# Key/value block of a two-layer trunk: all eight weight slabs fetched at once, products by feature group

## The reference

```python
def rms_norm(x, g):
    y = x * lax.rsqrt(jnp.mean(x * x, axis=-1, keepdims=True) + NORM_EPS)
    return y * g

a = rms_norm(h, g[0])                      # h = x, (256, 2048)
qkv = a @ w_qkv                            # (2048, 2048 + 256 + 256)
q = qkv[..., :2048]; k = qkv[..., 2048:2304]; v = qkv[..., 2304:]
# sliding-window attention with sinks, @ w_o, added to h; then a squared-ReLU MLP;
# layer 1: a gated MLP over chunks, added to h; then a squared-ReLU MLP
```

## Time and profile before

| | |
|---|---|
| median of 3 runs | 1972.24 us (1971.83 to 1972.36) |
| the profiled execution's span | 1971.5 us |
| PE busy | 1949.2 us, 99% of the span, 8914 products and transposes |
| PE weight loads | 1604.2 us, 81% |
| DVE busy / ACT busy | 1076.2 us (55%) / 972.2 us (49%) |
| granted TensorE clock, mean | 0.997 |
| moved by DMA | 368.40 MB, 187 GB/s on average |

### The profile page before, as it was taken

How to read it: one execution, slowest core, us unless ns; L and a number is a source line. 1 busy time by engine, 2 the same in 40 slices (tenths; PEclk the granted TensorE clock), 3 DMA queues, 4 the chain that set the end, 5 groups by cost and what they waited for, 6 DMA issues and landing times.

```text
span 1971.5 us, 26643 instructions
## 1 busy us (share of the span) xinstructions
PE 1949.2 (99%) x8914; PEld 1604.2 (81%) x8914; DVE 1076.2 (55%) x1276; ACT 972.2 (49%) x1339; POOL 6.2 (0%) x23
## 2 busy tenths in 40 slices
PE   7999999999999999999999999999999999999998
PEld 5777888888888888888888888888888888888886
DVE  5666575454454455455667655654544554544455
ACT  6666465435434543454564445654355435434542
POOL 0000000000000000000000000000000000000000
PEclk9999999999999999999999999999999999999999
DMA  6634656555555555555475555565555555555553
GB/s 205 203 128 164 207 197 203 191 192 182 191 195 180 189 192 192 192 172 196 150 259 171 192 189 177 173 212 199 194 177 188 196 191 190 178 199 189 182 192 107
DMA packets 189833, 368.40 MB, mean 187 GB/s; under 512 B 12616, under 2 KB 12752, under 8 KB 189008
## 3 DMA queue, kind: packets, MB, share of 16 engines
q1 hardware_dynamic: 187264, 360.75, 54.8%
q0 software_dynamic: 1040, 6.82, 0.9%
q10 hardware_dynamic: 1472, 0.08, 0.0%
HBM read 365.51 MB, written 2.10 MB: 186 GB/s over the span
## 4 chain that ended last, share of the span: by engine, by line
PE 98%; DMA 1%; ACT 0%; DVE 0%; SPq 0%; issue 0%; DVEq 0%; ACTq 0%
PE acc L357 31%; PE acc L359 31%; PE acc L358 31%; PE t L378 2%; DMA w_raw<-in_attn_w_qkv 1%; PE t L391 1%; PE scores L459 0%; PE o L481 0%; PE t L469 0%; PE scores L591 0%; PE t L439 0%; ACT a_hi L650 0%; DVE w_lo L977 0%; DVE h L1014 0%; ACT w_hi L630 0%
## 5 line engine op out<-in xcount | busy, mean ns | idle before, releaser
L977 DVE TENSOR_TENSOR w_lo<-w_raw,w_hi 128x1024 fp32r<-128x1024 f32 x680 | 820.6, 1224 | 632.1 <-ACT w_hi L630 603.5
L630 ACT ACTIVATE w_hi<-w_raw 128x1024 fp32r<-128x1024 f32 x680 | 708.4, 1058 | 626.0 <-PE acc L359 590.9
L357 PE MATMUL acc<-w_hi,a_hi 128*128 128x512 f32 x1440 | 573.5, 398 | 4.8 <-DVE w_lo L977 4.4
L359 PE MATMUL acc<-w_hi,a_lo 128*128 128x512 f32 x1440 | 563.2, 391 | 0.0
L358 PE MATMUL acc<-w_lo,a_hi 128*128 128x512 f32 x1440 | 562.5, 391 | 0.0
L357 PE MATMUL acc<-w_hi,b_hi 128*128 128x512 f32 x1280 | 500.9, 391 | 0.0
L359 PE MATMUL acc<-w_hi,b_lo 128*128 128x512 f32 x1280 | 498.4, 389 | 0.0
L358 PE MATMUL acc<-w_lo,b_hi 128*128 128x512 f32 x1280 | 498.1, 389 | 0.0
L357 PEld LDWEIGHTS acc<-w_hi,a_hi 128*128 128x128 f32 x1440 | 271.3, 188 | 62.2 <-issue 7.5
L359 PEld LDWEIGHTS acc<-w_hi,a_lo 128*128 128x128 f32 x1440 | 271.2, 188 | 58.3
L358 PEld LDWEIGHTS acc<-w_lo,a_hi 128*128 128x128 f32 x1440 | 271.6, 189 | 53.5
(11 more groups left out here) (120 smaller groups left out, 475.6 us busy)
## 6 DMA issues: line engine op xcount, KB each, us to landing
w_raw<-in_mlp_w_up SPq DMA_DIRECT2D x256, 512.0 KB, 4.2
w_raw<-in_mlp_w_down SPq DMA_DIRECT2D x256, 512.0 KB, 4.4
w_raw<-in_sgu_w_in SPq DMA_DIRECT2D x64, 512.0 KB, 4.6
w_raw<-in_attn_w_qkv SPq DMA_DIRECT2D x40, 512.0 KB, 4.6
w_raw<-in_attn_w_o SPq DMA_DIRECT2D x32, 512.0 KB, 4.2
w_raw<-in_sgu_w_out SPq DMA_DIRECT2D x32, 512.0 KB, 4.4
gain<-in_norm_gains POOLq DMA_DIRECT2D x4, 1024.0 KB, 5.4
h<-in_x SPq DMA_DIRECT2D x8, 256.0 KB, 11.4
```

The costliest lines, as they stand in the source:

```text
L357: nc.tensor.matmul(acc[t][:, :], lhsT=x_hi[:, kb, tok], rhs=w1, start=(kb == 0), stop=False)
L359: last = nc.tensor.matmul(acc[t][:, :], lhsT=x_lo[:, kb, tok], rhs=w1, start=False, stop=(kb == KB - 1))
L630: nc.scalar.activation(w_hi[:, i % SLOTS, :], w_raw[:, i % RAW_SLOTS, :], ACT.Copy).then_inc(hi_made, 1)
L977: nc.vector.tensor_tensor(w_lo[:, i % SLOTS, :], w_raw[:, i % RAW_SLOTS, :], w_hi[:, i % SLOTS, :].bitcast(F32), ALU.subtract).then_inc(lo ...
```

## The change

In the key/value block alone:

- Slabs 4 to 7 go to four slots in y (kv_raw) with four semaphores of their own (kv_landed). SP issues all 16 transfers, x units and slabs in turn, with no wait. Query slabs 0 to 3 then wait for DVE's low part of key/value slabs 0 to 3.
- Units come by feature group, both halves of a group one after the other (X_UNIT). PE multiplies, for each pair, both its slabs with t 0, then both with t 1, with the next group's two transposes after the second and the third slab half.
- ACT and DVE take unit i, slab i, for i from 0 to 7. Only then come ACT's four squares, each followed by the split of a query slab (0 to 3), the root, kv_evac(0), query slab 4, kv_evac(1), query slab 5. DVE's sum for the norm stands behind query slab 3's low part.
- The branches for layer 0 in `first_block` go; the other blocks keep their order.

The diff, without the branches that go:

```diff
+X_UNIT = [(pair, t) for pair in range(NB) for t in range(TOK)]
...
+        kv_raw = yf[:, :].rearrange("p (i n) -> p i n", i=RAW_SLOTS)
...
+        kv_landed = [sem(f"kv_landed{i}") for i in range(RAW_SLOTS)]
...
+        def raw(blk, i):
+            if isinstance(blk, int) and blk == B_KV and i >= RAW_SLOTS:
+                return kv_raw[:, i - RAW_SLOTS, :]
+            return w_raw[:, i % RAW_SLOTS, :]
...
             def load_x(n):
-                pair, t = UNIT[n]
+                pair, t = X_UNIT[n]
...
-            for units, slabs in (([0], (0, 2)), ([1], (2, 3)), ([2, 3], (3, 4)), ([4], (4, 6)), ([5, 6, 7], (6, 8))):
-                for n in units:
-                    load_x(n)
-                load_block(B_KV, w_qkv[0], D, slabs=range(*slabs))
-            with sp.Fori(0, NB) as j:
+            for i in range(2 * PAIRS):
+                load_x(i)
+                sp.dma_start(raw(B_KV, i).rearrange("p (k n) -> p k n", k=SLAB_KB), kv_source(i)
+                             ).then_inc(slab_landed[i] if i < RAW_SLOTS else kv_landed[i - RAW_SLOTS], 16)
+            for i in range(RAW_SLOTS):
+                sp.wait_ge(lo_made, i + 1)
+                src = w_qkv[0].rearrange("(k p) n -> p k n", p=P)[:, i * SLAB_KB:(i + 1) * SLAB_KB, 0:COL]
+                sp.dma_start(w_raw[:, i, :].rearrange("p (k n) -> p k n", k=SLAB_KB), src).then_inc(slab_landed[i], 16)
+            load_block(B_Q, w_qkv[0], 0, slabs=range(RAW_SLOTS, 2 * PAIRS))
+            with sp.Fori(1, NB) as j:
                 load_block(j + B_Q, w_qkv[0], j * COL)
...
+            def kv_block():
+                transpose_unit(0, 0, True)
+                transpose_unit(1, 0, True)
+                for pair in range(PAIRS):
+                    for t in range(TOK):
+                        for i in (2 * pair, 2 * pair + 1):
+                            pe.wait_ge(t_lo, X_UNIT.index((pair, t)) * 4 + (i % 2 + 1) * SLAB_KB)
+                            multiply_slab(B_KV, a_hi, a_lo, i, t)
+                            if pair < PAIRS - 1 and (t, i % 2) in ((0, 1), (1, 0)):
+                                transpose_unit(2 * pair + 2 + t, 0, True)
...
-            first_block(B_KV, 0, first_layer=True)
+            kv_block()
...
+            def kv_block(evac):
+                for i in range(2 * PAIRS):
+                    split_unit(i, 0, 0, X_UNIT)
+                    split_slab(B_KV, i)
+                for i, (t, part) in zip((2, 3, 4, 5), ((0, 0), (1, 0), (0, 1), (1, 1))):
+                    for pair in (2 * part, 2 * part + 1):
+                        act.wait_ge(x_landed[X_UNIT.index((pair, t))], 16)
+                    square_h(t, part)
+                    split_next(B_KV, i)
+                take_root()
+                act.wait_ge(norm_done, norms[0])
+                evac(0)
+                split_next(B_KV, 6)
+                evac(1)
+                split_next(B_KV, 7)
...
-            first_block(B_KV, 0, 0, kv_evac, layer0=True)
+            kv_block(kv_evac)
...
+            def kv_block():
+                for i in range(2 * PAIRS):
+                    split_unit(i, 0, 0, X_UNIT)
+                    split_slab(B_KV, i)
+                split_next(B_KV, 2, 3, 4, 5)
+                input_norm()
+                rotary_angles()
+                split_next(B_KV, 6, 7)
...
-            first_block(B_KV, 0, 0, layer0=True)
+            kv_block()
```

More of the change, by code:

```diff
@@ L381, in transpose_unit @@
             def transpose_unit(n, use0, first_layer=False):
-                pair, t = UNIT[n]
+                pair, t = X_UNIT[n] if first_layer else UNIT[n]
                 if first_layer:
@@ L421, in first_block @@
                     if step in units:
-                        transpose_unit(units[step], use0, first_layer)
-                h_base[0] += 0 if first_layer else UNITS
+                        transpose_unit(units[step], use0)
+                h_base[0] += UNITS
             h_base = [0]
@@ L625, in split_slab @@
             def split_slab(blk, i):
-                act.wait_ge(slab_landed[i % RAW_SLOTS],
-                            blk * (32 * PAIRS // RAW_SLOTS) + 16 * (i // RAW_SLOTS + 1))
+                if not isinstance(blk, int) or blk > B_KV:
+                    act.wait_ge(slab_landed[i % RAW_SLOTS],
+                                blk * (32 * PAIRS // RAW_SLOTS) + 16 * (i // RAW_SLOTS))
+                elif i < RAW_SLOTS:
+                    act.wait_ge(slab_landed[i], 16)
+                else:
+                    act.wait_ge(kv_landed[i - RAW_SLOTS], 16)
                 at_least(act, slab_used, blk * (2 * PAIRS) + (i + 1 - SLOTS))
[L630 to L634, removed]
+                nc.scalar.activation(w_hi[:, i % SLOTS, :], raw(blk, i), ACT.Copy).then_inc(hi_made, 1)
             def split_next(blk, *slabs):
@@ L642, in split_ahead, with split_unit @@
                 split_next(blk, 2 * pair, 2 * pair + 1)
-            def split_unit(n, use0, norm):
-                pair, t = UNIT[n]
+            def split_unit(n, use0, norm, order=UNIT):
+                pair, t = order[n]
                 act.wait_ge(t_filled, use0 + n + 1)
@@ L675, in first_block @@
+            def first_block(blk, use0, norm, evac):
                 h0 = h_seen[0]
-                h_seen[0] += 0 if layer0 else UNITS
+                h_seen[0] += UNITS
                 def square(t, part):
[L679 to L684, removed]
-                    square_h(t, part)
@@ L687, in first_block @@
[L687 to L691, removed]
+                    act.wait_ge(h_ready, h0 + UNIT.index((2 * part + 1, t)) + 1)
+                    square_h(t, part)
                 split_unit(2, use0, norm)
[L693 to L696, removed]
+                split_ahead(blk - 1, 3)
@@ L711, in first_block @@
                 square(1, 1)
-                if not layer0:
-                    split_next(blk, 3)
+                split_next(blk, 3)
                 take_root()
@@ L976, in split_slab @@
                 dve.wait_ge(hi_made, blk * (2 * PAIRS) + (i + 1))
-                nc.vector.tensor_tensor(w_lo[:, i % SLOTS, :], w_raw[:, i % RAW_SLOTS, :],
+                nc.vector.tensor_tensor(w_lo[:, i % SLOTS, :], raw(blk, i),
                                         w_hi[:, i % SLOTS, :].bitcast(F32), ALU.subtract).then_inc(lo_made, 1)
-            def split_slabs(blk, pair):
-                for i in (2 * pair, 2 * pair + 1):
-                    split_slab(blk, i)
             def split_next(blk, *slabs):
@@ L1026, in inverse, with input_norm @@
                 nc.vector.reciprocal(dst[:, tok], root[:, tok]).then_inc(norm_done, 1)
[L1028 to L1060, removed]
+            def input_norm():
                 sums[0] += 2 * TOK
@@ L1065, in first_block @@
                 inverse(r_in)
-                if layer0:
-                    rotary_angles()
+            def kv_block():
[6 more added lines that the diff above has]
+                split_next(B_KV, 6, 7)
+            def first_block(blk, use0, norm):
+                split_unit(2, use0, norm)
+                split_ahead(blk - 1, 3)
+                update_h(4)
+                split_unit(3, use0, norm)
+                update_h(5)
+                split_unit(4, use0, norm)
+                update_h(6)
+                split_next(blk, 0)
+                split_unit(5, use0, norm)
+                split_next(blk, 1)
+                update_h(7)
+                split_unit(6, use0, norm)
+                split_next(blk, 2)
+                split_unit(7, use0, norm)
+                split_next(blk, 3)
+                input_norm()
                 split_ahead(blk, 2)
```

18 lines of the change are left out of this document (7 added, 11 removed).

## The result

The changed kernel takes 1977.81 us (median of 9 runs) against 1972.24 for the kernel before (9 runs): 5.6 us more, a ratio of 1.0028 with a 95% interval of 1.0019 to 1.0037. Forecast were 1978.2 us, with 1975.4 to 1981.2 as the range. The profiled execution spans 1977.7 us, 6.2 more than before. A time is 1.8 us above its execution's span (1979.53 for the 1977.7 here), so the profiled executions lie above their medians, by 1.7 us after, as the longest of the 9, and by 1.1 us before.

A forecast was written before the change was run, and what follows sets the result against it. TensorE was taken to bound the kernel, the query block's start being what the change can move. Starting 3.6 us later plus 2.4 us of fallen clock gives +6.0: 1978.2 us, range 1975.4 to 1981.2.

The forecast's parts named there:

- The anchor: Key/value block: slab 3 lands at 20.7 us again and PE takes it at 23.1, so this start doesn't move.
- the transfers' part: Part 1, key/value block: removing SP's waits for slabs 4 to 7 is worth nothing.
- Case (d): Transfers come earlier without SP's waits, slab 3 starts at 21.3 us, not 23.1: +4.2, 1976.4 us; chance 0.08.
- The loop: Part 2, key/value block: transposes, units and slabs take 7.7 us a pair against PE's 6.3, so PE waits 1.4 in each.
- evac(0): ACT's step that frees acc 0 for the query block: starts at 47.6 us, after squares, query splits and norm.
- The clock: Part 4: PE's clock falls once, at the wait before the query block, costing 2.4 us at half rate.
- the prediction's own sign: Granted clock near 0.6 in 45 to 50 or 50 to 55 and 1.00 in 25:30; below 1 in both is (b).
- rival (b): The clock falls both times, also at the wait before slab 3: +8.2, 1980.4 us; chance 0.20.
- The sum: Whole kernel: 3.6 us later query block plus 2.4 of clock, +6.0; span 1977.5, time 1978.2 us; chance 0.52.
- part 3: ACT frees acc 0 at 48.7 us; the query block starts at 48.8, 3.6 later, after a 6.2 us PE wait.
- Rival (a): The clock stays at its upper level through the 6.2 us wait before the query block: +3.6, 1975.8 us; chance 0.15.
- (c): evac(0) isn't late and the query block starts at 42.7 us: -2.5, 1969.7 us; chance 0.05.

The follow-up runs named there:

- e2: Kernel before with only the transfers changed: slabs 4 to 7 go to y, same order of issue, no waits on SP; 1972.16 us, ratio 1.0000.
- e3: Changed kernel with slabs 4 to 7 back in the four raw slots with their waits, x units and slabs still in turn; 1977.10 us, ratio 1.0027.
- e7: Changed kernel with the attention sinks loaded as one row of 128 bytes per partition instead of pieces of 8 bytes; 1976.06 us, ratio 1.0023.
- e5: Changed kernel with 20 extra products on PE between the key/value block and the query block, filling the wait; 1975.09 us, ratio 1.0016.
- e1: Changed kernel with only ACT's and DVE's order moved: squares and root earlier, evac(0) behind query slab 1; 1970.06 us, ratio 0.9989.
- e4: Changed kernel with evac(0) ahead of the splits of query slabs 2 and 3, norm's sum ahead of their low parts; 1973.98 us, ratio 1.0012.
- e9: Kernel before with the transfers without waits (slabs 4 to 7 in y) and the sinks loaded as one row; 1964.70 us, ratio 0.9963.

## Why the prediction was right, point by point

**The anchor.** Slab 3's first product was to be near 23.1 and is at 22.88. e2 and e3 take the transfers' part out of the sum from both sides (1972.16 and 1977.10). Case (d) is out as to its cause: slab 3 landed at 20.40. In e7 slabs do land early, and +4.1 was measured where (d) says +4.2. That the two agree is in part luck: slab 3 starts at 20.35 and not at 21.3, and the query block at 45.40 and not at 47.0. The wait in front of slab 3 was put at 2.1 us and is 2.9 (19.97 to 22.88), since unit 3, expected at about 18, was transposed at 16.70.

**The loop.** ACT starts units 4 and 6 at 26.57 and 34.41, 7.8 us apart for a forecast of 7.7, idle 5.1 and 3.8 before them, where 3.5 was forecast for both; the 5.1 has the half rate behind slab 3 in it. PE's waits at slabs 4 and 5 read 0.40 and 0.55, where 0.7 each was forecast; the idle time in the brackets is counted from the modelled end of the product before, 0.39 us behind its start, while the pace is 0.23, so 0.16 is to be added to each.

**evac(0).** The forecast put it at 47.6, it began at 48.41. Term by term: slab 3's anchor -0.2. Half rate from 22.9 to 26 us, +1.7 (with the anchor, unit 4 at 26.57 for 25.1). The loop, +0.1. Four squares and splits, 38.32 to 46.3, are 8.0 and not 8.8: **this term was mis-sized**. The 1.24 of a square was taken from a row with a unit behind it, and that unit started at 35.38, just as its transpose ended (34.75 + 0.60): a wait for PE was read as ACT's own time. With a split behind it the next step comes 1.04 later (38.32 to 39.36). Low part, norm and root, 46.40 to 48.41, as worked out. The wait was 5.0 us, forecast 6.2: the block ended 1.9 us later and evac(0) 0.8 later.

**The clock.** Nine products at half rate, 49.51 to 53.52, are 4.0 us for 2.05: 2.0 lost, forecast 2.4. e5 takes this fall alone away and gains 2.4 us in the median. The forecast said that the clock falls once and reads 1.00 in 25:30; in the profiled execution it reads 0.79 and 0.87 in 20:25 and 25:30 and fell twice, which by the prediction's own sign is rival (b). (b)'s price was too high: +8.2 in all, for a difference of the spans of 6.2. The clock fell near slab 3 in the traces of the changed kernel and of e5, and not in those of e1, e3 and e4, which have the same products up to there. How often it did in the changed kernel's other eight executions isn't known, and so it stays open whether the median is one with one fall or with two.

**The sum.** The query block starts 4.3 us later (forecast 3.6), and with 2.0 behind it this is 6.2, the difference of the spans. The median of the runs is 5.6 above, for 6.0 forecast. The mechanism of part 3 is as forecast; that the figure fits so well is partly luck. In the profiled execution 1.7 us of half rate behind slab 3, which was given to rival (b), stand against a term 0.8 too large and the fall in front of the query block, 0.4 cheaper than forecast. The 0.7 us that the sum put around the span is 1.8 in every execution listed; the +6.0 doesn't depend on it, the forecast span of 1977.5 does. Rival (a) is out by the windows around 50 us, (c) by the 4.98 us wait. e1 has what (c) names, evac(0) in time: the kernel is faster than before, by 2.3 us (2.5 forecast).

## What to carry to other kernels

When work is regrouped, follow each engine's list to the step that frees the next stage's buffer: here four squares and four splits for later use stood ahead of one read-out, and 5 us of TensorE and its clock paid for them. Waits of an issuing engine need not be worth anything: here their removal gave nothing, neither behind a queue full of transfers (e2) nor where the products no longer waited for slabs (e9). Look at how long the issues themselves take, and whether anything waits for what they fetch, before you buy slots to remove waits. And if transfers are slow in one stretch, look for small pieces on another queue there: two loads of 4 KB in pieces of 8 bytes cost the kernel before 7 us, more than the 2.6 that the prediction gave the new order. In the changed kernel, whose waits lay elsewhere, the same edit gave 1.5.

## What the runs showed of the hardware that was not expected

The two loads of sinks, 4 KB each, share the 16 DMA engines with the slabs: 1142 packets in 15 us, with 3.6% of the engines' time, went with 212 GB/s in all, and 274 packets with 358. The Trainium skill (DMA: Bandwidth & Descriptors, Queues, rings and completion order) says that each engine goes round its queues a packet at a time, which fits; the rate lost is far more than the small packets' own share of the time, and why is left open.

Where the granted clock fell, and where it didn't: it was down at the end of waits of 4.40 us (before), 5.17 (e2), 4.98 (after), 5.01 (e3) and 5.00 (e7), and up at the end of waits of 1.98 (e4, 44.01) and 2.13 (e3, 22.00). Behind the wait of 2.75 (after, 22.88) the second product came after 0.51 us, the next ones after 0.43. Behind the wait of 2.15 (e5, 21.82) four products still ran 0.23 to 0.30 us apart, and the half rate began at 22.8, one microsecond after the wait had ended. So 2.13 and 2.15 us came out differently, in two kernels; what decides isn't shown. With e4's two groups of times it is likely, but not shown, that one kernel can have executions with and without the half rate, and that this is a part of the spread of the changed kernel's runs (1976.8 to 1979.5, with mean clocks of 0.997 and 0.998).

The clock column doesn't tell everything. In the changed kernel's first products, from 9.64 to 12.33 us, the pace is 0.43 us, that of half rate, and the windows from 5 to 15 show a granted clock of 1.00:

```profile
10.00:15.00 5.00, 5.00 (x19) 3.98 (x19) 1.66 (x4) 0.83 (x3) 0.00 (x0) 1.00 0.58 172
```

```profile
11.05 0.63 PE L375 MATMUL acc<-w_hi,a_hi 128*128 128x512 f32 x1
11.48 0.63 PE L376 MATMUL acc<-w_lo,a_hi 128*128 128x512 f32 x1
```

Why the column misses it isn't known. The distance of the products' starts is the surer sign.
